# Merging three gated branches by pairs of tiles, with tanh gates computed between attention units, and a start and an end cut into pieces

## The chip, the cores and the metric

The kernel runs on one core of one Trainium2 chip. The metric is the device time of one execution in microseconds (us). The times of the kernel before are the median of three runs; the trace comes from a separate, profiled execution.

## The reference

The input is one sequence of 256 tokens with 1024 features, and a memory of the same size. Two models run one after the other, both two layers deep. A layer of the first ("encoder") is a SwiGLU feed-forward, a mixer of stick-breaking attention and a gated delta rule, a cross attention, and a second feed-forward, each added to the running `h` after an RMS norm. The second ("decoder", its layers are called layer 0 and layer 1 here) is what the largest part of the change touches:

```python
def hybrid_layer(x, ...):
    h = rms_norm_2(x, norm_g)
    proj = h @ w_in                       # q, k, v of three branches, z gates, gl (3 x 1024 columns)
    ...
    y_moba = (o_moba * jax.nn.silu(mz)) @ w_up_moba      # 384 -> 1024
    y_nsa = (o_nsa * jax.nn.silu(nz)) @ w_up_nsa         # 256 -> 1024
    y_fox = (o_fox * jax.nn.silu(fz)) @ w_up_fox         # 384 -> 1024
    g = jax.nn.sigmoid(gl + b_gate).reshape(B, S, 3, D_MODEL)
    merged = g[:, :, 0] * y_moba + g[:, :, 1] * y_nsa + g[:, :, 2] * y_fox
    return x + merged @ w_out
```

Everything is fp32. With 256 tokens the selections of the sparse attentions take in all blocks, so the kernel computes plain causal attention for each.

## The kernel before

**Layout.** Features lie on the 128 partitions, tokens (256) along the free axis. A vector of 1024 features is 8 tiles of 128x256; two tiles share one PSUM bank (128x512), and such a pair of tiles is called a pair here. `h` is the running sum, `xs` the normed input of a block.

**Matmuls.** Each product of fp32 values is made of three fp32r matmuls: a value is split in a rounded high part and the rest, its low part, and high x high, high x low and low x high are added. So every weight block (128x128) takes three matmuls of 256 columns. Weights come from HBM as 560 units of 8 blocks (512 KB), through a ring of 10 slots (`ring`). ACT copies each unit to its rounded high part (`w_hi`, 6 slots, `highs`, L1025); DVE subtracts to get the low part in place (`w_lo`, `lows`, L1439). PE counts `unit_begun` when it starts a unit, and this frees slots for the DMA queue of SP and for `w_hi`. `ahead(u)` on ACT and DVE says how far ahead of unit u the splits are made: 5 units on ACT, 4 on DVE.

**Order.** There is no scheduler. Each engine has its own instruction stream, written by hand (`ffn_pe`, `hybrid_act`, `hybrid_dve` and so on), and they meet in counted semaphores: `need(sig, k)` waits until signal `sig` was told k times. An instruction that waits holds all that stand behind it on its engine.

**The start.** SP issues the whole input `x` into `h`, the first 136 columns of the constants, the norm gains `enc_par`, and ten units of weights. PE, ACT, DVE and POOL all wait until the first three have landed (`loaded`). ACT then makes the high parts of six units, and only after them the high parts of `xs` (L1409) and the squares (L1411); DVE makes the low parts of `xs` (L1449) and sums the squares. PE runs the first projection with `first_pair` (L448 to L453): a bank's two tiles, features 0 to 5 of both first and then 6 and 7, so that it can begin before the input is complete. `token_sums` (L461) then takes the sums over the features, and the second projection follows (L383 to L387, `project`).

**The attention units of a hybrid layer.** 20 units of attention (6 moba, 8 nsa, 6 fox) run as a pipeline: PE scores, DVE scale, mask and row maximum (L1897 to L1903), ACT exp (L1359, L1361), DVE normalize, PE transpose, ACT copy `pt` (L1374), PE values, and DVE makes the branch outputs `ob` (8 tiles: 3 moba, 2 nsa, 3 fox). PE fills its waits with the projection of the gates (`filler`), which DVE scales and stores into `gts` (`gates`, L1838, signal `gl_e`, 12 pairs).

**The merge** follows the units. PE runs 12 projections, branch by branch: 4 pairs of moba (18 matmuls each), 4 of nsa (12), 4 of fox (18), in four banks. ACT first computes all 24 gate tiles with sigmoid (L1378), then splits units, waits for each projection, and last makes the high parts of the merged tiles (`mg_hi`, L1387). DVE multiplies each projection with its gate (L1944, L1946), adds it to the sum (L1948), splitting units in between, and at the end makes the 8 low parts (`mg_lo`, L1951), each after its `mg_hi`. A merged pair is complete only with the fox projection of that pair. PE then runs the output projection (4 banks of 48 matmuls, `project(..., "mg_lo")`), and `next_dve` adds each bank to `h` (L1483).

**The end.** After the last sum SP stores all of `h` with one DMA.

## Time and profile before

| what | value |
|---|---|
| median of 3 runs | 2070.9 us (2070.31 to 2077.01) |
| the profiled execution, its own time | 2071.85 us |
| its span, first to last instruction | 2070.1 us |
| busy: PE / PEld / DVE / ACT | 1950.9 / 1812.1 / 1270.7 / 969.8 us |
| chain that ended last, by engine | PE 86%, DVE 8%, ACT 3%, issue 2% |
| mean granted clock of TensorE | 0.985 |
| HBM read | 299.30 MB, 145 GB/s over the span |

PE is busy 94% of the span, so time can only come from the 6% in which it stands, or from where its granted clock is low. PEld is the weight load of TensorE, PEclk the clock that was granted (1.00 is 2.4 GHz, 0.50 is 1.2 GHz). A bracket in a timeline row, [2.04 <-DVE arena L1903], is the idle time of the engine before that row and what ended it. Most buffers of the merge lie in one SBUF tensor, `arena`, which is the name that the rows show.

### The profile page before, as it was taken

What the parts mean: (1) busy time and instruction counts of PE and PEld (TensorE: products, weight loads), DVE (VectorE), ACT (ScalarE), POOL (GpSimd) and SP (SyncE); (2) the same over time, 40 slices, a digit from 0 to 9 for tenths busy, and PEclk for the clock granted to TensorE, in tenths of its full rate; (3) what the DMA queues carried; (4) which work ended last, traced back from release to release, by engine and by line L of the source; (5) the groups of instructions that cost most, each with busy time, mean ns of one, the idle gap of its engine ahead of it and who ended that gap; (6) DMA issues with size and microseconds to landing.
All of it is one profiled execution on the core that took longest, in us unless ns stands there. A gap on an engine that the chain in (4) does not pass through costs nothing.

```text
span 2070.1 us, 35095 instructions
## 1 busy us (share of the span) xinstructions
PE 1950.9 (94%) x14810; PEld 1812.1 (88%) x14810; DVE 1270.7 (61%) x2085; ACT 969.8 (47%) x1481; POOL 79.2 (4%) x68
## 2 busy tenths in 40 slices
PE   6999997888999999999889989999999998999997
PEld 6999996887999999999768879999898778898777
DVE  5775574454666567665744637666754778645775
ACT  5544555244544454454542545435544455544452
POOL 0000101300000000000003000000000000000000
PEclk9999998999999999999999999999999999999999
DMA  7555431222444555544221324555445224445221
GB/s 293 184 190 187 163 123 61 72 102 92 171 183 181 208 184 183 184 180 156 102 82 62 122 92 184 185 190 186 143 156 191 82 91 146 151 162 184 82 92 62
DMA packets 83742, 302.63 MB, mean 146 GB/s; under 512 B 9089, under 2 KB 11393, under 8 KB 83201
## 3 DMA queue, kind: packets, MB, share of 16 engines
q1 hardware_dynamic: 83584, 300.39, 40.6%
q8 instruction: 117, 1.92, 0.4%
q14 instruction: 41, 0.33, 0.0%
HBM read 299.30 MB, written 1.05 MB: 145 GB/s over the span
## 4 chain that ended last, share of the span: by engine, by line
PE 86%; DVE 8%; ACT 3%; issue 2%; DMA 0%; SPq 0%; DVEq 0%; ACTq 0%
PE bank L383 22%; PE bank L387 21%; PE bank L386 21%; PE bank L657 3%; DVE w_lo L1439 2%; PE bank L401 2%; PE bank L404 2%; PE bank L405 2%; PE bank L837 1%; PE bank L950 1%; PE bank L772 1%; PE bank L448 1%; PE bank L452 1%; PE bank L453 1%; PE bank L915 1%
## 5 line engine op out<-in xcount | busy, mean ns | idle before, releaser
L383 PE MATMUL bank<-xs,w_hi 128*128 128x256 f32 x2576 | 737.6, 286 | 4.6 <-issue 4.1
L1439 DVE TENSOR_TENSOR w_lo<-ring,w_hi 128x1024 fp32r<-128x1024 f32 x544 | 653.1, 1234 | 122.2 <-ACT w_hi L1025 121.3
L1025 ACT ACTIVATE w_hi<-ring 128x1024 fp32r<-128x1024 f32 x544 | 565.1, 1053 | 345.1 <-PE bank L383 275.7
L387 PE MATMUL bank<-xs,w_lo 128*128 128x256 f32 x2576 | 724.3, 281 | 0.0
L386 PE MATMUL bank<-xs,w_hi 128*128 128x256 f32 x2576 | 724.3, 281 | 0.0
L383 PEld LDWEIGHTS bank<-xs,w_hi 128*128 128x128 f32 x2576 | 488.0, 189 | 25.2 <-issue 20.5
L386 PEld LDWEIGHTS bank<-xs,w_hi 128*128 128x128 f32 x2576 | 488.0, 189 | 3.1 <-issue 2.9
L387 PEld LDWEIGHTS bank<-xs,w_lo 128*128 128x128 f32 x2576 | 487.9, 189 | 0.0
L383 PE MATMUL bank<-a,w_hi 128*128 128x256 f32 x704 | 197.0, 280 | 0.0
L387 PE MATMUL bank<-a,w_lo 128*128 128x256 f32 x704 | 196.6, 279 | 0.0
L386 PE MATMUL bank<-a,w_hi 128*128 128x256 f32 x704 | 196.4, 279 | 0.0
L387 PEld LDWEIGHTS bank<-a,w_lo 128*128 128x128 f32 x704 | 132.3, 188 | 0.0
L383 PEld LDWEIGHTS bank<-a,w_hi 128*128 128x128 f32 x704 | 132.0, 188 | 0.0
L386 PEld LDWEIGHTS bank<-a,w_hi 128*128 128x128 f32 x704 | 131.8, 187 | 0.0
L1514 DVE TENSOR_TENSOR arena<-bank,rstd 128x256 f32<-128x256 f32 x88 | 37.3, 424 | 147.0 <-PE bank L387 142.2
L1086 ACT ACTIVATE arena<-arena 128x256 f32<-128x256 f32 x88 | 36.8, 418 | 174.0 <-DVE arena L1514 174.0
L1359 ACT ACTIVATE arena<-arena 128x128 f32<-128x128 f32 x40 | 16.1, 402 | 112.9 <-DVE arena L1903 112.9
L448 PE MATMUL bank<-xs,w_hi 128*128 128x256 f32 x128 | 37.0, 289 | 17.4 <-DVE xs L1449 16.8
L1695 DVE TENSOR_TENSOR arena<-arena,bank 128x512 f32<-128x512 f32 x24 | 16.4, 684 | 58.5 <-PE bank L657 58.5
L383 PE MATMUL bank<-mg,w_hi 128*128 128x256 f32 x128 | 37.6, 294 | 13.0 <-issue 13.0
L1478 DVE SCALAR_TENSOR_TENSOR arena<-bank,rstd 128x512 f32<-128x512 f32 (+1 forms) x20 | 11.7, 583 | 61.8 <-PE bank L387 61.8
L1055 ACT ACTIVATE xs<-h,enc_par 128x256 fp32r<-128x256 f32 x40 | 18.6, 504 | 62.1 <-DVE h L1481 44.2
(392 smaller groups left out, 3162.8 us busy)
## 6 DMA issues: line engine op xcount, KB each, us to landing
ring<-in_w SPq DMA_DIRECT2D x560, 512.0 KB, 3.2
arena<-in_mem SPq DMA_DIRECT2D x2, 1024.0 KB, 13.5
const<-in_const SPq DMA_DIRECT2D x1, 1647.0 KB, 16.3
h<-in_x SPq DMA_DIRECT2D x1, 1024.0 KB, 4.8
out<-h SPq DMA_DIRECT2D x1, 1024.0 KB, 3.9
dec_par<-in_dec SPq DMA_DIRECT2D x1, 615.0 KB, 19.5
enc_par<-in_enc SPq DMA_DIRECT2D x1, 165.0 KB, 4.7
const<-in_const SPq DMA_DIRECT2D x1, 68.0 KB, 4.7
```

The costliest lines, as they stand in the source:

```text
L383: last = nc.tensor.matmul(o, wh, hi(x, k0 + k), start=k == 0, stop=False, skip_group_check=True)
L386: nc.tensor.matmul(o, wh, lo(x, k0 + k), start=False, stop=False, skip_group_check=True)
L387: last = nc.tensor.matmul(o, wl, hi(x, k0 + k), start=False, stop=k == nk - 1, skip_group_check=True)
L401: last = nc.tensor.matmul(o, xh, wh, start=k == 0, stop=False, skip_group_check=True)
L404: nc.tensor.matmul(o, xl, wh, start=False, stop=False, skip_group_check=True)
L405: last = nc.tensor.matmul(o, xh, wl, start=False, stop=k == KD - 1, skip_group_check=True)
L448: last = nc.tensor.matmul(o, wh, hi(x, k), start=j == 0 and k == 0, stop=False, skip_group_check=True)
L657: last = nc.tensor.matmul(cut(bank[b], i), cut(lhs, c * GH + i), cut(rhs, c * GH + i), start=True, stop=True, skip_group_check=True)
L1025: nc.scalar.activation(w_hi[:, s * UNIT:(s + 1) * UNIT], ring[:, u % RU, :], AF.Copy).then_inc(sems("w_hi"), 1)
L1086: nc.scalar.activation(e, e, AF.Silu).then_inc(*a.tell('ff_e'))
L1439: nc.vector.tensor_tensor(w_lo[:, r * UNIT:(r + 1) * UNIT], ring[:, r, :], w_hi[:, s * UNIT:(s + 1) * UNIT].bitcast(F32), ALU.subtract).th ...
L1514: nc.vector.tensor_tensor(ebuf[:, f % 5, :], bank[f % 5][:, 0:T], rstd, ALU.mult).then_inc(*d.tell('g_r'))
```

## The change

1. **Merge by pair.** PE takes the 12 projections in the order of `UPS`: moba and nsa of pairs 0 and 1, then fox of 0 and 1, then all three of pair 2, then of pair 3. The weights are laid out in that order. DVE makes the low parts of a pair (`merged_low`) after projections 5, 6, 9 and 11 (counted from 0), and splits fewer units ahead from projection 6 on. ACT makes `mg_hi` of a pair as soon as it is summed.
2. **Gates as tanh.** sigmoid(v) = (1 + tanh(v/2))/2. ACT computes `tanh` with half the bias (`half_bg`, made by DVE), in the attention units, after `pt` (`gates_turned` says how many pairs by which unit). DVE multiplies with one fused op, (g + 1) * y, and the factor 1/2 goes into the split of `mg`. ACT loads the table set `exp_and_others` after the compression norm of a layer, in place of the sigmoid's.
3. **Output projection** begins with `first_pair`: of its first bank, features 0 to 5 of both tiles, then 6 and 7.
4. **The start.** SP issues `enc_par`, two tiles of `x`, unit 0, six tiles of `x`, unit 1, the constants, and then the other units. ACT and DVE work on the first two tiles as soon as they are there; ACT splits three units in between, not six before. Only what needs the constants waits for them.
5. **The end.** Five stores of 2, 2, 2, 1 and 1 tiles, each after its own sum.

The diff, cut to its core (`SHARED` only renames which signals share a semaphore):

```diff
@@ first_pair: the signal it waits for is a parameter @@
-        def first_pair(pe, w, x, b, tell):
+        def first_pair(pe, w, x, b, tell, each='x_lo', made=-KD):
@@ sync @@
-            for dst, src in ((h[:, :, :], arrays["x"]), (const[:, 0:FIRST], arrays["const"][:, 0:FIRST]),
-                             (enc_par[:, :, :], arrays["enc"])):
-                e.dma_start(dst, src).then_inc(sems("loaded"), 16)
-            for u in range(RU):
+            e.dma_start(enc_par[:, :, :], arrays["enc"]).then_inc(sems("loaded"), 16)
+            e.dma_start(h[:, 0:2, :], arrays["x"][:, 0:2, :]).then_inc(sems("loaded"), 16)
+            e.dma_start(ring[:, 0, :], arrays["w"][0]).then_inc(sems("landed0"), 16)
+            e.dma_start(h[:, 2:KD, :], arrays["x"][:, 2:KD, :]).then_inc(sems("loaded_x"), 16)
+            e.dma_start(ring[:, 1, :], arrays["w"][1]).then_inc(sems("landed1"), 16)
+            e.dma_start(const[:, 0:FIRST], arrays["const"][:, 0:FIRST]).then_inc(sems("loaded_const"), 16)
+            for u in range(2, RU):
...
-            sp.e.wait_ge(*sp.need('h', 5 * (4 * LAYERS + LAYERS)))
-            e.dma_start(out, h[:, :, :]).then_inc(sems("stored"), 16)
-            e.wait_ge(sems("stored"), 16)
+            done = 5 * (5 * LAYERS - 1)
+            for j, (k, n) in enumerate(((0, 2), (2, 2), (4, 2), (6, 1), (7, 1))):
+                sp.e.wait_ge(*sp.need('h', done + j + 1))
+                e.dma_start(out[:, k:k + n, :], h[:, k:k + n, :]).then_inc(sems("stored"), 16)
+            e.wait_ge(sems("stored"), 5 * 16)
@@ hybrid_pe @@
-                for br, (lo_, nk) in enumerate(((0, 3), (3, 2), (5, 3))):
-                    pe.e.wait_ge(*pe.need('ob', lo_ + nk))
-                    for j in range(4):
-                        if m >= 4:
-                            pe.e.wait_ge(*pe.need('up_out', m - 3))
-                        project(pe, w, ob, nk, banks[m % 4], "up_full", k0=lo_)
-                        m += 1
+                for m, (j, br, _) in enumerate(UPS):
+                    first, nk = UP_TILES[br]
+                    pe.e.wait_ge(*pe.need('ob', first + nk))
+                    if m >= 4:
+                        pe.e.wait_ge(*pe.need('up_out', m - 3))
+                    project(pe, w, ob, nk, banks[m % 4], "up_full", k0=first)
...
-                    project(pe, w, mg, KD, b, "w_full", "mg_lo")
+                    if j == 0:
+                        first_pair(pe, w, mg, b, "w_full", "mg_lo", 0)
+                    else:
+                        project(pe, w, mg, KD, b, "w_full")
@@ hybrid_act @@
+                nc.scalar.preload_act_table_set("exp_and_others")
+                a.e.wait_ge(*a.need('half_bg', 1))
+                def gate_tanh(j):
+                    for c in (2 * j, 2 * j + 1):
+                        a.e.wait_ge(*a.need('gl_e', j + 1))
+                        nc.scalar.activation(gts[:, c, :], gts[:, c, :], AF.Tanh, bias=half_bg[:, c:c + 1],
+                            scale=0.5).then_inc(*a.tell('gl_s'))
...
-                a.e.wait_ge(*a.own())
-                for c in range(24):
-                    a.e.wait_ge(*a.need('gl_e', c // 2 + 1))
-                    nc.scalar.activation(gts[:, c, :], gts[:, c, :], AF.Sigmoid,
-                        bias=bgate[:, c:c + 1]).then_inc(*a.tell('gl_s'))
...
+                    for j in range(gates_turned(i), gates_turned(i + 1)):
+                        gate_tanh(j)
+                for j in range(gates_turned(n + 1), 12):
+                    gate_tanh(j)
+                for m, (j, br, used) in enumerate(UPS):
                     s.ahead(u0 + U_UP + used // UB)
-                    a.e.wait_ge(*a.need('up_full', j + 1))
-                for j in range(4):
-                    a.e.wait_ge(*a.need('mgd', j + 1))
-                    nc.scalar.activation(hi(mg, 2 * j, 2), mgf[:, 2 * j:2 * j + 2, 1, :], AF.Copy).then_inc(*a.tell('mg_hi'))
+                    a.e.wait_ge(*a.need('up_full', m + 1))
+                    if br == 2:
+                        a.e.wait_ge(*a.need('mgd', j + 1))
+                        nc.scalar.activation(hi(mg, 2 * j, 2), mgf[:, 2 * j:2 * j + 2, 1, :], AF.Copy,
+                            scale=0.5).then_inc(*a.tell('mg_hi'))
@@ scalar, start @@
-            e.wait_ge(sems("loaded"), 48)
+            nc.scalar.preload_act_table_set("natural_log_exp_and_others")
...
-            s.highs(HU)
+            e.wait_ge(sems("loaded"), 32)
             for j in range(4):
+                if j == 1:
+                    e.wait_ge(sems("loaded_x"), 16)
                 for k in (2 * j, 2 * j + 1):
...
+                if j != 1:
+                    s.highs(1 if j == 0 else j)
+            for j in range(4):
                 nc.scalar.activation(sq[:, 2 * j:2 * j + 2, :], h[:, 2 * j:2 * j + 2, :],
                     AF.Square).then_inc(*a.tell('x_sq'))
+            e.wait_ge(sems("loaded_const"), 16)
@@ hybrid_dve @@
-                        w.ahead(u0 + U_UP + used // UB)
...
-                for k in range(KD):
-                    d.e.wait_ge(*d.need('mg_hi', k // 2 + 1))
-                    nc.vector.tensor_tensor(lo(mg, k), mgf[:, k, 1, :], hi(mg, k).bitcast(F32),
-                        ALU.subtract).then_inc(*d.tell('mg_lo'))
+                def merged_low(j):
+                    d.e.wait_ge(*d.need('mg_hi', j + 1))
+                    for k in (2 * j, 2 * j + 1):
+                        nc.vector.scalar_tensor_tensor(out=lo(mg, k), in0=mgf[:, k, 1, :], scalar=0.5,
+                            in1=hi(mg, k).bitcast(F32), op0=ALU.mult, op1=ALU.subtract).then_inc(*d.tell('mg_lo'))
+
+                for m, (j, br, used) in enumerate(UPS):
+                    w.lows(u0 + U_UP + used // UB + (HU - 2 if m < 6 else 2))
+                    d.e.wait_ge(*d.need('up_full', m + 1))
+                    d.e.wait_ge(*d.need('gl_s', 2 * (4 * br + j) + 2))
...
+                    nc.vector.scalar_tensor_tensor(out=g if br else o, in0=g, scalar=1.0, in1=y, op0=ALU.add,
+                        op1=ALU.mult).then_inc(*d.tell('up_out'))
+                    if br:
+                        d.e.wait_ge(*d.own())
+                        nc.vector.tensor_tensor(o, o, g, ALU.add).then_inc(*d.tell('mgd' if br == 2 else None))
+                    if m in (5, 6, 9, 11):
+                        merged_low((5, 6, 9, 11).index(m))
@@ tables @@
+UP_TILES = ((0, 3), (3, 2), (5, 3))
+UPS, used = [], 0
+for j, br in ((0, 0), (0, 1), (1, 0), (1, 1), (0, 2), (1, 2), (2, 0), (2, 1), (2, 2), (3, 0), (3, 1), (3, 2)):
+    used += 2 * UP_TILES[br][1]
+    UPS.append((j, br, used))
+def gates_turned(i):
+
+    return min(12 * i // (len(UNITS) + 1), 4 + gate_steps(max(i - 1, 0)) // 4)
```

What stands where. ACT at the end of the attention units of layer 0 and in its merge, before (`arena<-arena 128x128` and `128x256` of L1359 and L1361 are the exps of a unit, `arena<-bank 128x384` its `pt`, L1378 the sigmoids, L1387 `mg_hi`):

```order
L1359 ACTIVATE arena<-arena 128x128
L1361 ACTIVATE arena<-arena 128x256
L1025 ACTIVATE w_hi<-ring 128x1024
L1374 ACTIVATE arena<-bank 128x384
L1025 ACTIVATE w_hi<-ring 128x1024
L1374 ACTIVATE arena<-bank 128x384
L1378 ACT_TABLE_LOAD
L1378 ACTIVATE arena<-arena,dec_par 128x256 x24
L1025 ACTIVATE w_hi<-ring 128x1024 x8
L1387 ACTIVATE mg<-arena 128x2x256 x4
```

The same place of the change (L1374, L1376 are the exps, L1389 `pt`, L1360 the tanhs, L1399 `mg_hi`):

```order
L1374 ACTIVATE arena<-arena 128x128
L1376 ACTIVATE arena<-arena 128x256
L1031 ACTIVATE w_hi<-ring 128x1024
L1389 ACTIVATE arena<-bank 128x384
L1360 ACTIVATE arena<-arena 128x256 x2
L1031 ACTIVATE w_hi<-ring 128x1024
L1389 ACTIVATE arena<-bank 128x384
L1360 ACTIVATE arena<-arena 128x256 x2
L1031 ACTIVATE w_hi<-ring 128x1024 x3
L1399 ACTIVATE mg<-arena 128x2x256
L1031 ACTIVATE w_hi<-ring 128x1024
L1399 ACTIVATE mg<-arena 128x2x256
```

The 24 sigmoids in a row are gone; two tanhs stand behind the `pt` of a unit, here of the last two, no table load stands between them and the exps, and `mg_hi` comes between the splits.

DVE at the end of the merge of layer 0, before (L1439 splits a unit, L1946 is the product, L1948 the sum, L1951 the low parts, L1483 the first sum into `h`):

```order
L1946 TENSOR_TENSOR arena<-bank,arena 128x512
L1948 TENSOR_TENSOR arena<-arena 128x2x256
L1439 TENSOR_TENSOR w_lo<-ring,w_hi 128x1024
L1946 TENSOR_TENSOR arena<-bank,arena 128x512
L1948 TENSOR_TENSOR arena<-arena 128x2x256
L1951 TENSOR_TENSOR mg<-arena,mg 128x256 x8
L1439 TENSOR_TENSOR w_lo<-ring,w_hi 128x1024 x2
L1483 SCALAR_TENSOR_TENSOR h<-bank,h 128x512
```

and of the change, from the low parts of pair 2 on (L1458 splits, L1965 is the product, L1969 the sum, L1956 the low parts, L1502 the sum into `h`):

```order
L1956 SCALAR_TENSOR_TENSOR mg<-arena,mg 128x256 x2
L1458 TENSOR_TENSOR w_lo<-ring,w_hi 128x1024
L1965 SCALAR_TENSOR_TENSOR arena<-arena,bank 128x512
L1969 TENSOR_TENSOR arena<-arena 128x2x256
L1458 TENSOR_TENSOR w_lo<-ring,w_hi 128x1024
L1965 SCALAR_TENSOR_TENSOR arena<-arena,bank 128x512
L1969 TENSOR_TENSOR arena<-arena 128x2x256
L1956 SCALAR_TENSOR_TENSOR mg<-arena,mg 128x256 x2
L1458 TENSOR_TENSOR w_lo<-ring,w_hi 128x1024 x4
L1502 SCALAR_TENSOR_TENSOR h<-bank,h 128x512
```

Only two low parts are left behind the last sum, and four splits, not two, stand before the first sum into `h`.

ACT at the start, of the change (L1424 `xs`, L1031 a split, L1429 the squares; before, it was six splits, then four times two `xs` and one square):

```order
L1417 ACT_TABLE_LOAD
L1424 ACTIVATE xs<-h,enc_par 128x256 x2
L1031 ACTIVATE w_hi<-ring 128x1024
L1424 ACTIVATE xs<-h,enc_par 128x256 x4
L1031 ACTIVATE w_hi<-ring 128x1024
L1424 ACTIVATE xs<-h,enc_par 128x256 x2
L1031 ACTIVATE w_hi<-ring 128x1024
L1429 ACTIVATE sq<-h 128x512 x4
L1031 ACTIVATE w_hi<-ring 128x1024 x4
```

The first `xs` stand ahead of the first split, and the squares behind the third.

## Rows read from the trace of the kernel before

**Rows 1.** Waits of PE, whole span: us in total, times, longest.

```profile
PE bank L383 <- issue: 17.2, 4, 6.5
PE bank L448 <- DVE xs L1449: 16.8, 1, 16.8
```

**Rows 2.** Windows: layer 1, gap after the merge, restart, last three projections.

```profile
core 0: us, PE busy (x) PEld busy (x) DVE busy (x) ACT busy (x) POOL busy (x), PEclk, DMA share, GB/s
2033.57:2040.08 6.51, 0.00 (x0) 0.03 (x1) 6.41 (x10) 2.29 (x4) 0.00 (x0) 0.82 0.00 0
2040.00:2044.70 4.70, 4.62 (x22) 4.65 (x23) 4.60 (x9) 1.37 (x2) 0.00 (x0) 0.51 0.02 3
...
2048.05:2065.00 16.95, 16.92 (x144) 16.72 (x142) 4.34 (x5) 1.06 (x1) 0.00 (x0) 1.00 0.00 1
```

**Rows 3.** Chain of waits: the merge's first matmul, layer 0 and layer 1.

```profile
1699.39 0.32 PE bank L383
...
2008.77 0.32 PE bank L383
```

**Rows 4.** Waits of ACT, attention units of layer 1, 1925 to 2009 us.

```profile
ACT arena L1359 <- DVE arena L1903: 45.5, 15, 4.4
```

**Rows 5.** Timeline of ACT, layer 1: start us, us, what, idle before it.

```profile
1936.79 0.40 ACT L1359 ACTIVATE arena<-arena 128x128 f32<-128x128 f32 x1 [2.04 <-DVE arena L1903]
...
2007.81 1.28 ACT L1378 ACT_TABLE_LOAD   x1
2009.11 9.71 ACT L1378 ACTIVATE arena<-arena,dec_par 128x256 f32<-128x256 f32 x24
...
2039.68 0.63 ACT L1387 ACTIVATE mg<-arena 128x512 fp32r<-128x512 f32 x1 [1.83 <-DVE arena L1948]
```

**Rows 6.** Timeline of DVE, layer 1: merge and last projections.

```profile
2009.59 0.43 DVE L1929 TENSOR_TENSOR ob<-arena,ob 128x256 fp32r<-128x256 f32 x1
...
2019.80 1.23 DVE L1439 TENSOR_TENSOR w_lo<-ring,w_hi 128x1024 fp32r<-128x1024 f32 x1 [5.86 <-ACT w_hi L1025]
...
2038.95 0.69 DVE L1948 TENSOR_TENSOR arena<-arena 128x512 f32<-128x512 f32 x1
2039.57 2.76 DVE L1951 TENSOR_TENSOR mg<-arena,mg 128x256 fp32r<-128x256 f32 x8
...
2048.05 0.69 DVE L1483 SCALAR_TENSOR_TENSOR h<-bank,h 128x512 f32<-128x512 f32 x1 [3.45 <-PE bank L387]
...
2065.01 0.76 DVE L1483 SCALAR_TENSOR_TENSOR h<-bank,h 128x256 f32<-128x256 f32 x2 [4.96 <-PE bank L387]
```

**Rows 7.** Timeline of DVE, layer 0: sums into h after its merge.

```profile
1738.12 0.69 DVE L1483 SCALAR_TENSOR_TENSOR h<-bank,h 128x512 f32<-128x512 f32 x1 [2.90 <-PE bank L387]
...
1755.37 0.75 DVE L1483 SCALAR_TENSOR_TENSOR h<-bank,h 128x256 f32<-128x256 f32 x2
```

**Rows 8.** Timeline of the start: ACT, DVE and PE.

```profile
8.39 1.28 ACT L1025 ACT_TABLE_LOAD   x1 [8.39 <-DMA ring<-in_w]
9.68 4.84 ACT L1025 ACTIVATE w_hi<-ring 128x1024 fp32r<-128x1024 f32 x5
10.85 1.22 DVE L1439 TENSOR_TENSOR w_lo<-ring,w_hi 128x1024 fp32r<-128x1024 f32 x1 [10.85 <-ACT w_hi L1025]
14.70 1.06 ACT L1025 ACTIVATE w_hi<-ring 128x1024 fp32r<-128x1024 f32 x1 [0.17 <-DMA ring<-in_w]
...
16.45 0.61 ACT L1411 ACTIVATE sq<-h 128x512 f32<-128x512 f32 x1
16.77 0.55 PE L448 MATMUL bank<-xs,w_hi 128*128 128x256 f32 x1 [16.77 <-DVE xs L1449]
...
24.12 0.88 DVE L1467 TENSOR_TENSOR ssum<-ssum,sq 128x256 f32<-128x256 f32 x2
...
26.20 0.39 PE L383 MATMUL bank<-xs,w_hi 128*128 128x256 f32 x1 [0.44 <-DVE w_lo L1439]
```

**Rows 9.** DMA issue of the store: count, KB, us to landing.

```profile
out<-h SPq DMA_DIRECT2D x1, 1024.0 KB, 3.9
```

More of the change, by code:

```diff
@@ L444, in first_pair @@
                     for k in ks:
[L445 to L446 removed]
+                        if pe.new(each, k + 1 + made):
+                            pe.e.wait_ge(*pe.need(each, k + 1 + made))
                         wh, wl, first = w.two()
```

52 lines of the change are left out of this document (17 added, 35 removed).

## The prediction, on record before the changed kernel ran

> **What bounds the kernel.** PE is busy 94% of the span, so I looked first for where it stands. The waits of PE over the whole span name two things that the change touches [rows 1]: one wait of 16.8 us before the first matmul, and a wait of line 383 of which the longest is 6.5 us. The windows place the long one: from 2033.57 to 2040.08 PE does nothing, and from 2040.00 to 2044.70 its granted clock is 0.51, that is 1.2 GHz instead of 2.4 GHz; behind that it is 1.00 again [rows 2]. This is the seam between merge and output projection in layer 1; layer 0 has the same seam. The timelines say who is late. ACT works 9.71 us on 24 sigmoids when the merge has just begun, splits no weights meanwhile, and DVE stands 5.86 us for a split [rows 5, 6]. DVE is then behind for the rest of the merge: its last sum starts at 2038.95 and the low parts of all eight tiles come after it [rows 6]. The reader is to see that the PE gap is a debt of DVE, made by ACT.
>
> **The unit of account.** Three projections of 48 matmuls take 16.95 us [rows 2]: 0.1177 us per matmul, 5.65 us per projection. The 12 projections of a merge are 4 x (18 + 12 + 18) = 192 matmuls, 22.6 us when nothing waits, and the first output projection ends 28.25 us after the merge began.
>
> **Merge, before.** The merge began at 1699.39 and at 2008.77 [rows 3]. The first sum into h, which starts when the first output projection ends, began at 1738.12 and 2048.05 [rows 6, 7]. So this stretch took 38.7 us in layer 0 and 39.3 us in layer 1, against 28.25: there is 10.5 and 11.0 us to be had, restart at the low clock included.
>
> **Merge, after.** Times from the merge's begin. *ACT:* the sigmoids and their table load (1.28 us) leave the merge. The last pair of tanhs is behind the last `pt`, which in before ended just ahead of 2007.81, so it is done near 0.1 even if a tanh takes the 0.40 us of a sigmoid (9.71 / 24) [rows 5]; no projection's product waits for it. *DVE:* a split costs about 1.13 us, a product and the sum behind it about 0.7 each. Until projection 9 DVE has less to do than PE: 10 products, 6 sums, 4 splits, 6 low parts are 7.0 + 4.2 + 4.5 + 2.1 = 17.8 us in the 19.1 us that PE takes for the same. The output tile of the last units (2009.59 plus 0.43, that is 1.25) is there long before the first fox projection, at 7.1 [rows 6]. *The tail:* projection 10 ends at 20.5. Behind it DVE has split (21.6), product (22.3), sum (23.0), split (24.1), product (24.8), sum (25.5); then ACT makes `mg_hi` in 0.63 (26.1) [rows 5], and two low parts of 0.345 each (2.76 / 8 [rows 6]) end at 26.8. PE leaves the merge at 22.6 and has 36 matmuls of features 0 to 5 of both tiles, until 26.8; it wants feature 6 then, which is there at 26.5, and feature 7 at 27.2. The four splits behind the low parts give the third unit of the output weights at 27.9; PE wants it at 28.25. So the seam closes, with 0.3 to 0.4 us to spare. The bounds of what is left are 0 and one split, one product and one sum more than I count, 2.5 us; I take 0.3 per layer, near the lower, since each duration comes from the same operation in the same stage. With no gap there is no low clock behind it. Gain 10.5 + 11.0 - 0.6 = 20.9 us.
>
> **Late next.** DVE comes 3 us late to the first sum into h. In layer 0 it had 2.90 us idle there [rows 7] and some more later, and the next layer begins with 4.2 us of matmuls that don't need the last sum. I cost that at nothing; with that cover gone it is 1 to 2 us, once.
>
> **Tanh in the units.** 12 pairs of 0.8 us per layer move into ACT's idle time before the exps. That is 45.5 us in 15 waits, 3.0 us each, in most of a layer's units [rows 4], and one of the shortest is 2.04 [rows 5]. Each unit gets at most one pair, behind its `pt`, where only the next exp is queued. So 0.8 fits under 2.0, and I cost it at 0; bounds 0 and, if the cover did not count, 9.7 us per layer. The table load for the exps and tanhs replaces the sigmoid's and stands before a wait of ACT: 0. `half_bg` is one tiny DVE operation per layer: 0.
>
> **Start.** ACT got going at 8.39, when unit 0 had landed; it had to wait for unit 5 until 14.70 [rows 8]. Five units of 512 KB in 6.31 us are 415 GB/s, and I take transfers to land in order at this pace. By the shapes, unit 0 and what was issued ahead of it were 1024 + 68 + 165 + 512 = 1769 KB, now 165 + 256 + 512 = 933 KB: 2.1 us earlier, at 6.3. The first two tiles of x land 1.3 us before that, the rest of x at 8.2, unit 1 at 9.5, unit 2 at 10.9. The table load (1.28) is done before all this. ACT: split of unit 0 until 7.3; DVE's part 1.22 [rows 8]; PE starts at 8.6, not at 16.77. But the gain is read at the second projection (26.20), whose place behind `token_sums` now waits for the squares. ACT: six `xs` (0.40 each), two splits, squares (4 x 0.52) from 8.2: 2.4 + 1.9 + 2.1 = 6.4, so 14.7. DVE has the last split of the three at 13.8, then sums of 0.70, 0.70, 0.44, 0.44, 0.44 and small waits: 16.7 (in before these ended at 25.0). PE: 17 matmuls or so at the low clock as in before, the rest at the high one, would be done at 16.1, so the sums decide. Token sums 0.6, second projection at 17.3: it needs unit 2, split long before (in before it still waited, 0.44). Gain 8.9 us. Bounds: 6.9 if nothing lands before 8.39, and 10.1 if PE and not the sums decided. Weights further on do not run short: PE needs unit 10 at 17.3 + 8 x 2.8 = 39.9, and even behind the big constants, mem and dec it lands near 29.
>
> **End.** The store of 1024 KB takes 3.9 us [rows 9]; at 415 GB/s 2.5 of it is transfer. The last piece is 128 KB, 0.3 us, and the pieces ahead are out of its way or nearly so. Gain 2.2, and I take 2.1 for the queue. The lower bound is 1.4, with a piece of its own pace and one waiting behind the other. The Trainium skill, "DMA: Bandwidth & Descriptors" (Anatomy of one DMA and Rules for kernel authors), speaks against pieces: a DMA has about 2.0 us of fixed cost and at least 1 MiB is best. By that price the last piece takes 2.3 us, which gives 1.6 and a sum of 31.4.
>
> **Sum.** 8.9 + 20.9 + 2.1 = 31.9 us. Against the profiled execution (span 2070.1, own time 2071.85) that is a span of 2038.2; its own time stands 0.95 above the median, and I take the difference off the median: 2070.9 - 31.9 = **2039.0 us**.
>
> **Rivals.**
> - *Another wait at the seam.* The margin is 0.3 us per layer, and DVE's fused operation (g + 1) * y on a PSUM bank, 24 times, is not in the trace of before in this form. If each is slower by 0.1, or the two scalings by 1/2 take the 0.44 of an `xs` low part, PE stands 1 to 3 us per layer. For: DVE's stretch is tight. Against: the sums into h, of the same kind and size, take 0.69 [rows 6]. About 2043.
> - *The first tiles land no earlier.* All queued transfers share the DMA engines; if they advance together, ACT starts at 8.39 as before, the sums end 2.0 later: 2041. Against: unit 5 landed 6.3 us after unit 0 though all were queued within 6 us, so they come one after the other [rows 8].
> - *The tanhs are not hidden.* If ACT's idle time is needed by the chain of a unit, 24 x 0.8 = 19.3 us come back: 2058.
> - *Slower than before: the tables change inside the units.* If tanh and exp needed different sets, each of 24 pairs would bring two loads of 1.30 and 0.8 of work, 3.4 us, under idle times of 3.0. By the two bounds of the cover 0.4 to 3.4 us a pair would show, in the middle 1.9 or 46 us: 2085. From 1.33 us a pair on (31.9 / 24) the kernel is slower than before. Against: the order of the change has no load there. The Trainium skill, "ScalarE: Activation LUTs" (Table sets), puts tanh into `exp_and_others`, and prices a switch at 2.66 us with its drain, where the rows have 1.28 and the next operation 0.02 later [rows 5]; by its price a pair would show 3.1 us, and the time would be 2114.
> - *It doesn't do what it says:* fox of pair 0 needs all attention units, so the merge cannot begin earlier; only if DVE's order (splits first) keeps it behind, is the merge as long as before: 2060.
>
> **How the numbers follow.** Forecast 0.62, seam 0.17, transfers 0.10, tanhs 0.05, tables 0.02, merge as before 0.02, else 0.02. The forecast's own range is 2037 to 2041.5; the seam rival reaches 2045. I give 2035.5 to 2045.5, the lower end for a start that PE decides and no stall. A change below 0.3%, 6 us, can't be told from none: faster 0.96, same 0.01, slower 0.03.
>
> **What would show it.** PE's first matmul near 8.6 and the second projection near 17.3. No PE wait above 1 us in the merge, clock 1.00 there, 28 us from its begin to the first sum into h. No sigmoid rows; ACT's waits before exps of a tanh unit shorter by 0.8, attention units as long as before. The last store landing about 1.8 us after its issue. It would be wrong if the units became longer, or if a gap of several us with a low clock behind it were left at the seam.

## The result, and the profile after

The change runs in 2038.15 us (median of 4 runs, 2034.12 to 2040.07); the kernel before, run beside it, in 2070.61 (2068.75 to 2077.01). The ratio is 0.9843, 95% interval 0.9829 to 0.9857, so 32.5 us are gained where 31.9 were forecast. The profiled execution took 2038.23 us with a span of 2036.4; before, 2071.85 and 2070.1. The two spans differ by 33.7.

The page of the change, busy time by engine and chain by engine:

```profile
PE 1941.9 (95%) x14810; PEld 1804.3 (89%) x14810; DVE 1271.0 (62%) x2087; ACT 968.9 (48%) x1481; POOL 79.2 (4%) x68
...
PE 88%; DVE 7%; ACT 2%; issue 2%; DMA 0%; SPq 0%; DVEq 0%; ACTq 0%
```

The waits of PE over the whole span:

```profile
...
PE bank L448 <- DVE w_lo L1458: 10.2, 1, 10.2
PE bank L383 <- DVE w_lo L1458: 6.1, 2, 3.4
...
PE bank L383 <- issue: 4.1, 2, 2.1
```

These answer to [rows 1]: the wait of line 383 has shrunk from 17.2 us in 4 times to 4.1 in 2; the two of 6.5 us, one per seam, are gone. The wait before the first matmul is 10.2 us instead of 16.8, and what ends it is now a split of weights, no longer `xs`. One more wait of PE is gone, which stood inside the merge of the kernel before, once in each layer, until DVE had multiplied a projection and so given its bank back:

```profile
PE bank L383 <- DVE arena L1944: 2.8, 2, 1.4
```

Windows of the change over the merge of layer 1 and the begin of the output projection (stretch and its us, then PE, PEld, DVE, ACT and POOL busy with their instructions, the granted clock, DMA share and GB/s):

```profile
1988.30:2010.90 22.60, 22.60 (x200) 22.60 (x200) 20.59 (x33) 10.16 (x12) 0.00 (x0) 1.00 0.50 165
2010.90:2016.60 5.70, 5.62 (x48) 5.37 (x47) 4.91 (x7) 2.67 (x4) 0.00 (x0) 1.00 0.00 0
```

Where [rows 2] have 6.5 us without PE and then a clock of 0.51, PE is busy but for 0.1 us, at a clock of 1.00. DVE in the same stretch, which answers to [rows 6]:

```profile
...
2010.66 1.22 DVE L1458 TENSOR_TENSOR w_lo<-ring,w_hi 128x1024 fp32r<-128x1024 f32 x1
...
2012.51 0.69 DVE L1969 TENSOR_TENSOR arena<-arena 128x512 f32<-128x512 f32 x1
2013.96 0.76 DVE L1956 SCALAR_TENSOR_TENSOR mg<-arena,mg 128x256 fp32r<-128x256 f32 x2 [0.76 <-ACT mg L1399]
2014.64 4.63 DVE L1458 TENSOR_TENSOR w_lo<-ring,w_hi 128x1024 fp32r<-128x1024 f32 x4
2019.18 0.69 DVE L1502 SCALAR_TENSOR_TENSOR h<-bank,h 128x512 f32<-128x512 f32 x1
...
2027.60 0.69 DVE L1502 SCALAR_TENSOR_TENSOR h<-bank,h 128x512 f32<-128x512 f32 x1 [4.86 <-PE bank L387]
2033.24 0.76 DVE L1502 SCALAR_TENSOR_TENSOR h<-bank,h 128x256 f32<-128x256 f32 x2 [4.96 <-PE bank L387]
```

The last sum of the merge starts at 2012.51, with two low parts behind it instead of eight. DVE is still at work on splits when the first output projection has ended, and so starts the first sum into `h` late (2019.18), but it idles 4.86 us before the one at 2027.60: the debt costs nothing. In layer 0 the first sum is as late (1721.15, 31.7 us after the merge's begin) and DVE has less idle time behind it, but no wait of PE shows between that projection's end and 1760 us, and from the 48th matmul of its output projection to the merge of layer 1 it takes 270.4 us, against 270.9 before.

The start of the change (timeline of all engines, cut), which answers to [rows 8]:

```profile
0.73 1.28 ACT L1417 ACT_TABLE_LOAD   x1 [0.73 <-PEq L2241]
...
5.12 0.91 ACT L1424 ACTIVATE xs<-h,enc_par 128x256 fp32r<-128x256 f32 x2 [3.10 <-DMA h<-in_x]
...
7.70 1.06 ACT L1031 ACTIVATE w_hi<-ring 128x1024 fp32r<-128x1024 f32 x1 [1.68 <-DMA ring<-in_w]
8.79 1.23 DVE L1458 TENSOR_TENSOR w_lo<-ring,w_hi 128x1024 fp32r<-128x1024 f32 x1 [2.25 <-ACT w_hi L1031]
...
9.65 1.71 ACT L1424 ACTIVATE xs<-h,enc_par 128x256 fp32r<-128x256 f32 x4 [0.90 <-DMA h<-in_x]
...
10.16 0.55 PE L448 MATMUL bank<-xs,w_hi 128*128 128x256 f32 x1 [10.16 <-DVE w_lo L1458]
```

PE starts at 10.16, when the forecast had 8.6, and the second projection, a few rows on, at 18.81 against 26.20 before. The table load and the first `xs` are done before unit 0 is there; ACT stands 1.68 us for it.

**Where the time went.** Lead of the change over the kernel before, read where the same instruction starts in both traces (us):

| place | before | change | lead |
|---|---|---|---|
| second projection | 26.20 | 18.81 | 7.4 |
| first sum into h of the first feed-forward | 161.05 | 155.09 | 6.0 |
| merge of layer 0 begins | 1699.32 | 1689.50 | 9.8 |
| merge of layer 1 begins | 2008.70 | 1988.26 | 20.4 |
| last sums into h | 2065.01 | 2033.24 | 31.8 |
| end of the span | 2070.1 | 2036.4 | 33.7 |

The merge itself, from its first matmul to the 48th of the output projection: 38.5 and 39.0 us before, 28.3 and 27.6 now (the 48th is counted to its start), 21.6 less in the two together. Start 7.4, merges 21.6, store 1.9 (33.7 - 31.8) are 30.9. Of the 10.7 us by which layer 1 stood above 28.3 before, 6.5 were the gap, 2.1 stalls inside the merge and 2.1 the restart at the low clock. The other 2.8 us of the spans arose where the two kernels do the same; I come back to them.

### The profile page after: what moved, and what is told of

The parts are those of the page before. It is cut to its first block, busy times and chain, and to the rows that moved or that the text cites. A ratio compares the mean times of both kernels' runs of the same rounds, so it can differ in the third digit from the quotient of the medians.

```text
span 2036.4 us, 35117 instructions
## 1 busy us (share of the span) xinstructions
PE 1941.9 (95%) x14810; PEld 1804.3 (89%) x14810; DVE 1271.0 (62%) x2087; ACT 968.9 (48%) x1481; POOL 79.2 (4%) x68
## 4 chain that ended last, share of the span: by engine, by line
PE 88%; DVE 7%; ACT 2%; issue 2%; DMA 0%; SPq 0%; DVEq 0%; ACTq 0%
PE bank L383 22%; PE bank L387 22%; PE bank L386 22%; PE bank L663 3%; PE bank L401 2%; PE bank L404 2%; PE bank L405 2%; DVE w_lo L1458 1%; PE bank L843 1%; PE bank L956 1%; PE bank L448 1%; PE bank L452 1%; PE bank L453 1%; PE bank L778 1%; PE bank L921 1%
## 5 line engine op out<-in xcount | busy, mean ns | idle before, releaser
L1031 ACT ACTIVATE w_hi<-ring 128x1024 fp32r<-128x1024 f32 x544 | 565.4, 1052 | 330.8 <-PE bank L383 258.7
L1458 DVE TENSOR_TENSOR w_lo<-ring,w_hi 128x1024 fp32r<-128x1024 f32 x544 | 653.5, 1235 | 103.9 <-ACT w_hi L1031 103.0
L1374 ACT ACTIVATE arena<-arena 128x128 f32<-128x128 f32 x40 | 16.1, 402 | 97.2 <-DVE arena L1923 97.2
L448 PE MATMUL bank<-xs,w_hi 128*128 128x256 f32 x128 | 36.8, 287 | 10.2 <-DVE w_lo L1458 10.2
L401 PE MATMUL bank<-w_hi,xs 128*128 128x512 f32 (+2 forms) x128 | 43.9, 343 | 0.0
```

The costliest lines, as they stand in the source:

```text
L401: last = nc.tensor.matmul(o, xh, wh, start=k == 0, stop=False, skip_group_check=True)
L448: last = nc.tensor.matmul(o, wh, hi(x, k), start=j == 0 and k == 0, stop=False, skip_group_check=True)
L1031: nc.scalar.activation(w_hi[:, s * UNIT:(s + 1) * UNIT], ring[:, u % RU, :], AF.Copy).then_inc(sems("w_hi"), 1)
L1458: nc.vector.tensor_tensor(w_lo[:, r * UNIT:(r + 1) * UNIT], ring[:, r, :], w_hi[:, s * UNIT:(s + 1) * UNIT].bitcast(F32), ALU.subtract).th ...
```

## Experiments

Ratios are to the kernel before, run on the same chip in the same job, with the 95% interval.

**The three parts, each alone.** Three kernels take from the change only the start (its transfers and the order of ACT and DVE), only the merge (order of projections, tanhs, low parts by pair, `first_pair`), or only the stores, as the diff above has them. The third, for instance, is the kernel before with

```diff
-            sp.e.wait_ge(*sp.need('h', 5 * (4 * LAYERS + LAYERS)))
-            e.dma_start(out, h[:, :, :]).then_inc(sems("stored"), 16)
-            e.wait_ge(sems("stored"), 16)
+            done = 5 * (5 * LAYERS - 1)
+            for j, (k, n) in enumerate(((0, 2), (2, 2), (4, 2), (6, 1), (7, 1))):
+                sp.e.wait_ge(*sp.need('h', done + j + 1))
+                e.dma_start(out[:, k:k + n, :], h[:, k:k + n, :]).then_inc(sems("stored"), 16)
+            e.wait_ge(sems("stored"), 5 * 16)
```

> The kernel before with the new start alone. Theory (the parts add, each read at its own place in the trace): second projection near 18.8 instead of 26.2, 7.4 us earlier, and the rest as before; the total 6 to 10 us under the kernel before, because stages that the change does not touch drift by 1 to 3 us with the granted clock. Rival (the lead of the start is lost again in the encoder, where other chains decide): total within 3 us of before.

> The kernel before with the merge by pair, the tanh gates and the output projection by first_pair, start and store as before. Theory: from the merge's first matmul to the first output projection's end 28.3 us in both layers, 10.5 and 11 us less, and units of attention as long as before: 21 to 22 us under the kernel before. Rival (part of the gain seen in the full change comes from the other parts): under 19 us.

> The kernel before with the store in five parts alone. Theory: last matmul to the end of the span 3.2 us instead of 5.1, 1.9 us less; in the total hardly to be told from none (0.1%), so it is read from the trace. Rival (fixed costs of the pieces add up): 4.5 us or more from the last matmul to the end.

Start alone: 2063.50, ratio 0.9962 (0.9949 to 0.9976). Merge alone: 2047.77, 0.9889 (0.9871 to 0.9907). Stores alone: 2066.23, 0.9983 (0.9971 to 0.9995). With 2070.39 of before, these are 6.9, 22.6 and 4.2 us, 33.7 together against 32.5 for the change: the parts add up within their intervals. In the traces, the first has its second projection at 18.68, 7.5 earlier than before, and keeps these 7.5 us to the end of the span (2062.6 against 2070.1), the second its output projection's 48th matmul 28.3 us after the merge's begin in both layers, and the third this end:

```profile
2059.20 0.76 DVE L1485 SCALAR_TENSOR_TENSOR h<-bank,h 128x256 f32<-128x256 f32 x2 [4.75 <-PE bank L387]
```

Its span ends at 2062.4, 3.2 us later; before, it was 5.1 from 2065.01 [rows 6]. So the store is worth 1.9, which lies within the interval of the medians' 4.2 (1.0 to 6.0).

**Order of work against order of transfers at the start.** The change with SP's six first issues in the old order, and then the opposite: the new issues with the old order on ACT and DVE, which wait for all first loads.

```diff
@@ e4: sync @@
-            enc_par, h[0:2], ring 0, h[2:KD], ring 1, const
+            h[0:2], h[2:KD], const, enc_par, ring 0, ring 1
@@ e10: kernel before, with the new issues, merge and stores; all three engines at the start @@
-            e.wait_ge(sems("loaded"), 48)
+            e.wait_ge(sems("loaded"), 32)
+            e.wait_ge(sems("loaded_x"), 16)
+            e.wait_ge(sems("loaded_const"), 16)
```

(In the first, each name stands for its whole `dma_start`. In the second, ACT and DVE also have their old order of splits, `xs` and squares, and the table load behind the wait.)

> The full change, but the start's transfers issued in the old order (all of x, constants, gains, then the units); the order of work on ACT and DVE is the new one. Theory A (most of the start's gain is the order of work: xs before the six splits): first matmul near 10.9, second projection near 19.5, total within 1 us of the full change. Theory B (it is the order of the transfers): first matmul at 14 or later, total 4 us or more above the full change.

> The full change, but at the start only the transfers stand in the new order: all engines wait for gains, x and constants together, ACT splits six units before it makes the first xs, as before. Theory (the order of work is nearly all of the start's gain): ACT gets going near 10 us, first matmul at 17 or later, second projection near 27, total 8 us above the full change. Rival: first matmul at 14 or earlier.

With the old transfers: 2041.18, 0.9854 (0.9835 to 0.9873), second projection at 19.55. With the old order of work: 2048.44, 0.9892 (0.9873 to 0.9911), second projection at 28.84, later than before. ACT there:

```profile
11.31 1.28 ACT L1034 ACT_TABLE_LOAD   x1 [11.31 <-DMA const<-in_const]
12.60 5.79 ACT L1034 ACTIVATE w_hi<-ring 128x1024 fp32r<-128x1024 f32 x6
```

So 6.7 of the 7.4 us are there with the old order of transfers (26.20 to 19.55), and 0.7 come with the new one; alone, the new transfers cost 2.6, since `const` now lands late and everything waits for it. The 6.7 are the order of work on ACT and DVE together with what the first kernel keeps besides: waits for only what is needed, `x` in two transfers, and the table load of 1.28 us ahead of the landing (at 0.73 instead of 8.39). These were not tried one by one. Both totals lie further from the change than was expected: 3.0 us above it where 1 was allowed, and 10.3 (9.9 above the change again, run beside it) where 8 was.

**The tanhs behind the units.** One line puts all 12 pairs ahead of the merge, as the sigmoids were:

```diff
-    return min(12 * i // (len(UNITS) + 1), 4 + gate_steps(max(i - 1, 0)) // 4)
+    return 0
```

> The full change, but all 24 tanhs stand behind the attention units, where the sigmoids stood. Theory (the order by pair helps only if ACT is free to split when the merge begins): DVE waits for the split of the sixth merge unit until about 10.7 us after the merge's begin and stays behind; from the merge's first matmul to the first output projection's end 33 us or more instead of 28.3, total 9 to 12 us above the full change (about 2048). Rival (it is the order by pair that closes the gap, tanhs anywhere): 28 to 29 us, total within 2 us of the full change.

2046.49 (2041.35 to 2051.98), 0.9885 (0.9864 to 0.9906). ACT at the begin of the merge of layer 1, then PE's wait in layer 1 (1990 to 2045), then the window behind it:

```profile
1985.78 9.70 ACT L1360 ACTIVATE arena<-arena 128x256 f32<-128x256 f32 x24
1995.38 2.94 ACT L1031 ACTIVATE w_hi<-ring 128x1024 fp32r<-128x1024 f32 x3
```

```profile
PE bank L448 <- DVE w_lo L1458: 2.0, 1, 2.0
```

```profile
2011.91:2015.50 3.59, 3.58 (x19) 3.59 (x20) 3.52 (x5) 0.00 (x0) 0.00 (x0) 0.57 0.02 5
```

The gap is back, smaller, and in layer 1 with the low clock behind it; in layer 0 a gap of 2.0 us too is followed by 1.00. The 48th matmul comes 31.4 and 32.3 us after the merge's begin instead of 28.3 and 27.6, less than the 33 or more that was expected; the rival (28 to 29) is out. What ACT does at the begin of the merge is paid by PE at its end.

**Branches one after the other.** Tanhs stay in the units, but the projections go moba, nsa, fox for all pairs, and all low parts come after the last sum:

```diff
-for j, br in ((0, 0), (0, 1), (1, 0), (1, 1), (0, 2), (1, 2), (2, 0), (2, 1), (2, 2), (3, 0), (3, 1), (3, 2)):
+for j, br in [(j, br) for br in range(3) for j in range(4)]:
...
-                    if m in (5, 6, 9, 11):
-                        merged_low((5, 6, 9, 11).index(m))
+                for j in range(4):
+                    merged_low(j)
```

> The full change, but the projections of the merge in the old order, branch by branch, and the eight low parts behind the last sum; tanhs in the units. Theory (both halves of the merge edit are needed): PE stands 3 to 4 us at the seam in each layer, until the last sum and the first low parts, perhaps with a low clock behind it; 32 us per merge stretch, total 7 to 10 us above the full change. Rival (freeing ACT was enough): within 2 us of the full change.

2047.24, 0.9889 (0.9871 to 0.9907). DVE in layer 1, and PE's wait there:

```profile
2014.40 0.69 DVE L1969 TENSOR_TENSOR arena<-arena 128x512 f32<-128x512 f32 x1
2015.01 2.77 DVE L1956 SCALAR_TENSOR_TENSOR mg<-arena,mg 128x256 fp32r<-128x256 f32 x8
2017.69 4.63 DVE L1458 TENSOR_TENSOR w_lo<-ring,w_hi 128x1024 fp32r<-128x1024 f32 x4
```

```profile
PE bank L448 <- issue: 2.6, 1, 2.6
```

PE stands 2.6 us ahead of the first matmul on `mg`, in each layer, where 3 to 4 were expected, then runs through (48th matmul at 31.1 us). The clock is 1.00 behind this gap in both.

**Two smaller parts of the seam.** First, DVE splits as far ahead in the second half of the merge as in the first; second, the output projection takes all features of one tile, then of the other, instead of `first_pair`:

```diff
@@ e7 @@
-                    w.lows(u0 + U_UP + used // UB + (HU - 2 if m < 6 else 2))
+                    w.lows(u0 + U_UP + used // UB + (HU - 2))
@@ e8 @@
-                    if j == 0:
-                        first_pair(pe, w, mg, b, "w_full", "mg_lo", 0)
-                    else:
-                        project(pe, w, mg, KD, b, "w_full")
+                    project(pe, w, mg, KD, b, "w_full", "mg_lo" if j == 0 else None)
```

> The full change, but DVE splits four units ahead in the whole merge (two more splits stand before the last low parts). Theory (the margin at the seam is 0.4 us, and two splits of 1.13 less DVE's idle time push the low parts of the last pair past it): PE waits 1.3 to 2 us for the low parts in each layer, total 3 to 4 us above the full change. Rival (there is slack): no PE wait at the seam.

> The full change, but the first output projection runs tile by tile over all 8 features (weights laid out so). Theory: feature 6 is wanted 2.1 us after the merge's last matmul and is there 4 us after it; PE waits 1.8 to 2.2 us per layer, total about 4 us above the full change. Rival: no wait, the low parts are in time anyway.

Splits ahead: 2042.83, 0.9868 (0.9849 to 0.9887). No first pair: 2047.58, 0.9893 (0.9878 to 0.9907). The waits of PE at the seams of layer 0 and 1, of the first and then of the second kernel:

```profile
PE bank L448 <- DVE mg L1956: 1.9, 1, 1.9
...
PE bank L448 <- DVE mg L1956: 1.1, 1, 1.1
```

```profile
PE bank L383 <- DVE mg L1953: 2.1, 1, 2.1
```

(The last twice, alike.) The clock stays 1.00 behind three of these four. Behind the 1.9 us of layer 0 it falls:

```profile
1716.50:1719.90 3.40, 3.40 (x18) 3.40 (x18) 2.98 (x4) 1.28 (x3) 0.00 (x0) 0.50 0.00 0
```

The waits come to 3.0 and 4.2 us; the second kernel's median is 9.4 above the change's. Its trace says where about half of that arose: its merge of layer 0 begins at 1694.03, 4.5 us behind the change's 1689.50, in a part of the program that is the same in both (1.3 of it in the first feed-forward, 3.4 behind it with more time at the low clock; see the last section). All four of its runs (2046.33 to 2050.91) lie above all four of the change's, though, so whether this is chance stays open.

**The tanhs tripled.** Before each pair of tanhs, ACT computes two more of 128x512 of `h` into a scratch tile. Nothing reads them, so this adds work and leaves none out.

```diff
                 def gate_tanh(j):
...
+                    a.e.wait_ge(*a.own())
+                    for s_ in range(2):
+                        nc.scalar.activation(sq[:, 4 * s_ + 2 * (j % 2):4 * s_ + 2 * (j % 2) + 2, :], h[:, 0:2, :], AF.Tanh,
+                            scale=0.5).then_inc(*a.tell())
+                    a.e.wait_ge(*a.own())
```

> The full change with two more activations of 128x512 (Tanh of h into a free buffer) ahead of each pair of tanhs in the units, some 1.3 us more work of ACT per pair, 24 times. Theory (ACT's idle time before the exps, 2.0 to 4.4 us, covers the tanhs; 0.8 fits, 2.2 just about): 0 to 5 us above the full change, the waits of ACT before an exp shrink to near 0 in pair units. Rival (the pairs are only partly covered even now): about 31 us above it, 1.3 per pair.

2037.54 (2032.86 to 2041.90), 0.9842 (0.9819 to 0.9864): the change's time. ACT in a unit of layer 1 with a tanh, change and then tripled:

```profile
1971.26 0.90 ACT L1360 ACTIVATE arena<-arena 128x256 f32<-128x256 f32 x2
1974.69 0.40 ACT L1374 ACTIVATE arena<-arena 128x128 f32<-128x128 f32 x1 [2.54 <-DVE arena L1923]
```

```profile
1969.90 1.15 ACT L1360 ACTIVATE sq<-h 128x512 f32<-128x512 f32 x2
1971.09 0.91 ACT L1365 ACTIVATE arena<-arena 128x256 f32<-128x256 f32 x2
1973.20 0.40 ACT L1379 ACTIVATE arena<-arena 128x128 f32<-128x128 f32 x1 [1.21 <-DVE arena L1928]
```

The idle time before the exp takes all of it: 2.54 us becomes 1.21. Over the attention units of layer 1, ACT's waits before this exp are 45.5 us in the kernel before [rows 4], 39.2 in the change and 28.6 with the tanhs tripled.

**A finer start, and the change again.** One kernel goes on where the start is still open: unit 0 lands and is split in two halves of 512 columns, and in the first layer the token sums come behind the second projection (`ffn_pe(pe, w, 0 if l else 1)`), so that PE needn't wait for the squares.

```diff
-            e.dma_start(ring[:, 0, :], arrays["w"][0]).then_inc(sems("landed0"), 16)
+            e.dma_start(ring[:, 0, 0:512], arrays["w"][0][:, 0:512]).then_inc(sems("half_landed"), 16)
+            e.dma_start(ring[:, 0, 512:UNIT], arrays["w"][0][:, 512:UNIT]).then_inc(sems("landed0"), 16)
...
+                    if f == sums_after:
+                        token_sums(pe, 5, tall=False)
...
```

> The full change with the first unit of weights landing and split in two halves, and the token sums of the first feed-forward behind its second projection instead of ahead of it. Theory (the second projection waits for the sums, 0.9 us, and the first matmul for the low part of the first unit, 10.2): first matmul near 8.5, second projection near 16.3, no wait for the sums; 2.5 us less in the trace, total near 2035.6. Rival (ACT, held by the later sums, runs out of splits): a wait of PE for w_lo within the next 20 us takes it back.

> The full change again, unchanged, beside the finer start: 2036 to 2040, ratio 0.984.

Finer start: 2037.82 (2031.20 to 2040.69), 0.9839 (0.9813 to 0.9864). The change again: 2038.53 (2035.72 to 2041.59), 0.9852 (0.9828 to 0.9875). In the finer one PE starts at 7.76 and the second projection at 17.49:

```profile
7.76 0.55 PE L450 MATMUL bank<-xs,w_hi 128*128 128x256 f32 x1 [7.76 <-DVE w_lo L1997]
9.87 0.58 PE L450 MATMUL bank<-xs,w_hi 128*128 128x256 f32 x1 [0.49 <-DVE xs L1479]
```

That is 1.3 us earlier than in the change, of which the token sums behind it take back 0.6; what is left, 0.7, can't be told from nothing in the totals. The first matmul came earlier than expected (8.5), but the second projection 1.2 later (16.3). In the change, the first 15 matmuls come 0.21 us apart and the rest 0.12, from 13.3 on; here six come, PE stands 0.5 us for `xs`, and some 26 more come 0.21 apart, until 15.6. What was won at the first matmul is lost at this slower pace. No wait of PE for a split followed within 20 us, so the rival is out.

**The merge, free of what came before it.** From its first matmul in layer 1 to the end of the span, and the start of the 48th matmul of the output projection in layers 0 and 1 (us after the begin):

| kernel | to the end | 48th matmul |
|---|---|---|
| before | 61.4 | 38.5, 39.0 |
| start only | 61.4 | 38.5, 39.0 |
| merge only | 50.7 | 28.3, 28.3 |
| change | 48.1 | 28.3, 27.6 |
| change again | 48.2 | 27.6, 27.5 |
| tanhs tripled | 48.1 | 27.6, 27.6 |
| tanhs behind the units | 52.7 | 31.4, 32.3 |
| branches in a row | 51.5 | 31.1, 31.1 |
| splits ahead | 50.2 | 30.3, 29.6 |
| no first pair | 50.2 | 29.7, 29.7 |

Each part of the merge that is taken back costs 2.1 to 4.6 us here, so none is idle. Their sum is 12.2 (4.6 + 3.4 + 2.1 + 2.1), near the 11.4 that the change gains in this stretch without the store (61.4 - 48.1 - 1.9); that parts taken back one at a time add up is not shown, and they needn't.

## Why the prediction held, and where it didn't

**Start: forecast 8.9, measured 7.4.** The start is the term that was mis-sized, and the step of it that failed is "I take transfers to land in order at this pace". Windows of the change's first 8 us:

```profile
2.00:3.00 1.00, 0.00 (x0) 0.00 (x0) 0.00 (x0) 0.01 (x1) 0.00 (x0) 1.00 0.80 272
3.00:4.00 1.00, 0.00 (x0) 0.00 (x0) 0.00 (x0) 0.00 (x0) 0.00 (x0) 1.00 0.49 148
4.00:5.00 1.00, 0.00 (x0) 0.00 (x0) 0.00 (x0) 0.00 (x0) 0.00 (x0) 1.00 0.71 231
5.00:6.00 1.00, 0.00 (x0) 0.00 (x0) 0.34 (x1) 0.88 (x2) 0.00 (x0) 1.00 1.00 340
6.00:7.00 1.00, 0.00 (x0) 0.00 (x0) 0.54 (x2) 0.02 (x1) 0.00 (x0) 1.00 1.02 397
7.00:8.00 1.00, 0.00 (x0) 0.00 (x0) 0.00 (x0) 0.30 (x1) 0.00 (x0) 1.00 0.93 326
```

Not 415 but 148 to 397 GB/s. From 2.0 to 7.7 some 1.6 MB moved (the row sums), though unit 0 and what was issued ahead of it are 933 KB: later transfers took their share before unit 0 was complete. The trace of the kernel before has the same, which the forecast missed: its windows add up to 2.3 MB by 8.39 us, where 1769 KB were counted up to unit 0. The first two tiles of `x` came as forecast (5.12 for 5.0). Unit 0 came at 7.7, not 6.3, the rest of `x` at 9.65, not 8.2, and the 1.4 went through all that followed: PE's first matmul 1.6 late, the second projection 1.5. So the rival that transfers advance together was right in kind and in part; its full price, ACT starting at 8.39 as before, did not come. The engines' own steps held: six `xs`, two splits and the squares took from 9.65 to 16.1, 6.5 us for 6.4. That the sums of the squares and not PE decide held too: PE waits 0.9 us for them, and they end at 18.3 for 16.7.

**Merge: forecast 20.9, measured 21.6.** Both seams closed, and the list of waits has none of PE in either. The forecast's unit of 0.1177 us per matmul held in layer 0, with the 48th at 28.3 and next to no stall. In layer 1 the 192 matmuls of the merge came every 0.113 us, at a granted clock of 1.00 as well, and took 21.9 us instead of 22.7. So PE wanted feature 6 about 0.9 us sooner than I had it, and there the stall was, 0.24 us and 0.11 more at the next matmul, too short for the list:

```profile
2014.09 0.28 PE L453 MATMUL bank<-mg,w_lo 128*128 128x256 f32 x1
2014.44 0.39 PE L448 MATMUL bank<-mg,w_hi 128*128 128x256 f32 x1
```

The 48th came at 27.6. The merge-only kernel, which has 28.3 in both layers, gains 20.9; the 0.7 us more of the change are this pace, and not a merit of the edit (the change again, the same program, has 27.6 and 27.5). Why a merge takes one pace or the other is open. That 20.9 is the forecast's figure is in part luck: it read "before" at the sum into `h`, 0.24 us behind the 48th matmul's start in each layer, and "after" at the matmul, which made the gain some 0.4 too large, and the stall of 0.6 that it took off hardly came. The margins were as tight as forecast: low parts of the last pair were forecast to end at 26.8 after the begin and ended at 26.5 (2014.72 - 1988.26), and the edits that gave DVE more to do ahead of them, or let PE want them earlier, showed as waits of PE of 1.1 to 2.1 us. One sentence of the forecast was inconsistent: it asked for 28 us "from its begin to the first sum into h", while its own working put the four splits before that sum and DVE 3 us late. It is 31.7 and 30.9, as the working has it, and no wait of PE followed. The term "late next", put at nothing, held.

**The restart clock.** Forecast: no gap, no low clock. So it is. But a gap does not always bring it: in the kernel with late tanhs 2.0 us were followed by 0.57 in layer 1 and by 1.00 in layer 0, 1.9 us with splits ahead by 0.50, and 2.6 us with the branches in a row by 1.00.

**Tanhs: forecast 0, measured 0.** From the 48th matmul of layer 0's output projection to the merge of layer 1, which takes in that layer's attention units, it is 270.4 us for 270.9 before, and three times the tanhs' work changed neither the time nor the merge. ACT loads tables 25 times, as before, and there is no load between tanh and exp in a unit. The Trainium skill, "ScalarE: Activation LUTs" (Table sets), has tanh in the exps' set, and the trace agrees: 0.40 us from tanh to tanh and no reload. With that the slower rival falls. The rival that the chain of a unit needs ACT's idle time falls by the tripled tanhs.

**Store: forecast 2.1, measured 1.9.** The page's DMA issues of the change:

```profile
out<-h SPq DMA_DIRECT2D x3, 256.0 KB, 2.3
...
out<-h SPq DMA_DIRECT2D x2, 128.0 KB, 1.9
```

Three of the pieces have landed when the last one is issued at 2034.07; the fourth, issued 0.38 us ahead of it, is still under way. The last takes 1.9 us against 3.9 for the whole [rows 9]. The Trainium skill, "DMA: Bandwidth & Descriptors" (Anatomy of one DMA), has about 2.0 us of fixed cost per DMA on the path of GpSimd, while these are issued by SP. By that price the last piece would take 2.3 us as an estimate; it took 1.9, so the gain of 1.6 was 0.3 short, as mine was 0.2 over.

**The sum.** Terms 7.4 + 21.6 + 1.9 = 30.9 against 31.9. That the medians differ by 32.5, and the two profiled spans by 33.7, is not to the credit of the forecast: 2.8 us of the spans, and perhaps 1.6 of the medians, arose in stages that the change doesn't touch. They are in the range in which one kernel's runs differ (6 us among the four of the change). Of the 2.8, the stretch from the first sum into `h` to the merge of layer 0 gave 3.9, the first feed-forward took 1.4, and what is left is behind the merge of layer 0; the last section says where the first two come from. The start fell short by 1.5, the merge gave 0.7 more and this came on top: that the total lies within 1 us of the forecast is luck, and what can be credited is the terms, each read at its own place.

## What to carry to other kernels

When PE stands at a seam, look for the debt where it was made: here ACT's 24 sigmoids at the begin of a merge became a PE gap 25 us later. Move work that has no deadline into idle time further up; order the rest so that the last result needs the least behind it; then check that the engine that is late next has idle time before it matters. At this start, what the engines wait for and do first was worth more than what was sent first (6.7 us and 0.7), and a transfer's landing is not to be worked out from the full pace of the queue: the first microseconds are slower and shared. Where untouched stages drift by several microseconds, measure an edit from the nearest common instruction, not from the totals.

## What the runs showed of the hardware

The same stretch of program does not take the same time in each trace. The traces show two reasons.

**Stretches at half clock.** Where the granted clock isn't 1.00 it is 0.50 for some microseconds, and a window's 0.83 is a mean of both. In the change's trace each such stretch follows on waits of PE, as this one does:

```profile
1010.00:1017.00 7.00, 5.10 (x36) 4.32 (x34) 5.35 (x10) 3.56 (x6) 0.00 (x0) 1.00 0.20 75
1017.00:1027.00 10.00, 6.77 (x15) 3.58 (x16) 2.51 (x6) 6.60 (x10) 4.65 (x2) 0.50 0.00 0
```

Not all do. The merge-only kernel in layer 1, and then the change from the same matmul of the program on:

```profile
1823.20:1826.60 3.40, 3.40 (x27) 3.21 (x27) 0.00 (x0) 1.17 (x3) 0.00 (x0) 1.00 0.00 0
1826.60:1830.00 3.40, 3.40 (x17) 3.40 (x17) 2.67 (x7) 2.19 (x8) 1.70 (x2) 0.50 0.47 154
```

```profile
1820.17:1823.57 3.40, 3.40 (x30) 3.40 (x30) 2.67 (x7) 2.51 (x9) 1.71 (x2) 1.00 0.45 154
```

17 matmuls and 30 in the same time, with PE busy before and during both. The low clock stands at this place in six of the fourteen traces and not in the others; why is open. Summed over the windows of 10 us, the clock lost is 31.4 us before and 18.8 in the change, of which the seams hold a part.

This explains most of the drift. From the first sum into `h` of the first feed-forward to the merge of layer 0, the kernel before took 1538.3 us and lost 23.9 us of clock; the store-only kernel, the same there, 1533.4 and 17.1. The change took 1534.4 and lost 18.8; the change again 1530.3 and 13.7. Over all fourteen traces the time, 1530.3 to 1538.3, goes up with the clock lost, by some 0.7 us for each.

**Two paces at full clock.** The merge of layer 0 and of layer 1, in the change:

```profile
1690.00:1700.00 10.00, 10.00 (x88) 10.00 (x87) 8.69 (x13) 3.18 (x3) 0.00 (x0) 1.00 0.52 173
1990.00:2000.00 10.00, 10.00 (x90) 10.00 (x90) 9.29 (x12) 3.83 (x5) 0.00 (x0) 1.00 0.61 206
```

Inside one merge the pace is even, 0.118 us per matmul or 0.113. In the first feed-forward it is 0.117, 0.119 or 0.120, again even, at 1.00. So the stretch from the second projection to the first sum takes 134.9 us in most of the kernels, 136.3 in both profiled runs of the change (155.09 - 18.81 and 155.00 - 18.71) and in the one with the old order of transfers, and 137.6 in the one without first pair, whose program is the same there. That cost the change 1.4 of its 7.4 us in this run, and what sets the pace stays open.
